# RWKV-7 in eight chunks of 64 on 64x64 tiles of the array, its transitions made for all chunks at once, and the round reordered

## What is computed

```
w = -softplus(-(w0 + tanh(w_lr) @ w2)) - 0.5;  decay = exp(-exp(w))
a = sigmoid(a0 + a_lr @ a2)
kk = k * k_k;  kk = kk / max(norm(kk), 1e-12);  k = k * (1 + (a - 1) * k_a)
for each token:
    sa = state @ (-kk)
    state = state * decay + sa (x) (kk * a) + v (x) k
    y = state @ r
y = (y - mean(y)) * rsqrt(var(y) + eps) * ln_g + ln_b + sum(r * k * r_k) * v
```

## Time and profile before

| what | before |
|---|---|
| median of 3 runs | 1454.38 us (1452.08 to 1454.99) |
| profiled execution | 1457.13 us, span 1455.2 us |
| mean granted TensorE clock | 0.977 of full speed |
| PE busy | 1343.1 us, 92% of the span |
| DVE busy | 792.6 us, 54% |
| ACT busy | 555.6 us, 38% |
| POOL busy | 618.2 us, 42% |
| first `low_rank` (pair 0) starts | 101.0 us after the span's start |
| one steady round, `low_rank` to `low_rank` | 105.4 us |
| last round, its `low_rank` to the output projection's first product | 83.9 us |

### The profile page before, as it was taken

One profiled execution on the slowest core, in us unless ns is written; L12 is line 12 of the kernel. 1 busy time (PEld: TensorE's weight loads), 2 busy tenths in 40 slices (PEclk: granted clock), 3 DMA queues, 4 the chain that ended last, 5 costly groups with the idle time before them and its releaser, 6 DMA issues.

```text
span 1455.2 us, 24702 instructions
## 1 busy us (share of the span) xinstructions
PE 1343.1 (92%) x7914; PEld 1096.5 (75%) x7914; DVE 792.6 (54%) x1442; ACT 555.6 (38%) x1210; POOL 618.2 (42%) x584
## 2 busy tenths in 40 slices
PE   2999999999999999999999979899969999998995
PEld 1777878878878878878878858687847777776874
DVE  6546256366275274374383462205584777687357
ACT  4324344344254245254244354202242425435123
POOL 3634233242242341350351211477745656565772
PEclk9999999999999999999999989899989999999998
DMA  5212011111021120120120110333312222222331
GB/s 179 86 48 56 23 50 48 30 46 43 29 54 35 36 59 22 43 59 14 43 67 7 43 37 15 108 109 96 93 58 80 80 73 80 75 77 56 99 92 65
DMA packets 46688, 87.81 MB, mean 60 GB/s; under 512 B 5808, under 2 KB 6832, under 8 KB 46384
## 3 DMA queue, kind: packets, MB, share of 16 engines
q1 hardware_dynamic: 44352, 82.44, 19.7%
q10 hardware_dynamic: 2288, 4.72, 0.9%
HBM read 85.04 MB, written 2.10 MB: 60 GB/s over the span
## 4 chain that ended last, share of the span: by engine, by line
PE 72%; DVE 13%; issue 4%; ACT 4%; ACTq 0%; DVEq 0%
PE psum L272 67%; PE psum L426 3%; ACT mix L844 3%; DVE mix L1284 2%; DVE mix L1374 1%; DVE mix L1308 1%; ACT L844 1%; PE psum L781 1%; DVE mix L1746 1%; DVE mix L1664 1%; PE psum L351 1%; DVE mix L1457 1%; DVE mix L1675 1%; DVE mix L1738 1%; DVE mix L1729 1%
## 5 line engine op out<-in xcount | busy, mean ns | idle before, releaser
L272 PE MATMUL psum<-h_split,w_hi 128*128 128x512 f32 x2320 | 746.9, 404 | 17.1 <-DVE h_split L1288 9.2
L255 POOL TENSOR_SCALAR w_hi<-w_raw 128x512 fp32r<-128x512 f32 x290 | 205.3, 708 | 786.8 <-PE psum L272 668.4
L272 PEld LDWEIGHTS psum<-h_split,w_hi 128*128 128x128 f32 x2320 | 436.0, 192 | 127.7 <-issue 33.0
L272 PE MATMUL psum<-h_split,w_lo 128*128 128x512 f32 x1160 | 458.4, 395 | 0.0
L272 PE MATMUL psum<-mix 128*128 128x128 f32 (+4 forms) x3712 | 429.4, 287 | 28.4 <-ACT mix L844 11.7
L272 PEld LDWEIGHTS psum<-mix 128*128 128x128 f32 (+2 forms) x3712 | 369.6, 176 | 80.5 <-issue 33.8
L257 POOL TENSOR_TENSOR w_lo<-w_raw,w_hi 128x512 fp32r<-128x512 f32 x290 | 413.4, 1426 | 24.2
L844 ACT ACTIVATE mix<-psum 128x256 f32<-128x256 f32 (+4 forms) x620 | 229.2, 390 | 433.2 <-PE psum L272 241.1
L272 PEld LDWEIGHTS psum<-h_split,w_lo 128*128 128x128 f32 x1160 | 221.8, 191 | 48.4
L1374 DVE COPY_PREDICATED mix<-mask,psum 128x128 f32<-128x128 uint8 (+3 forms) x344 | 133.0, 431 | 171.0 <-PE psum L272 166.4
L844 ACT ACTIVATE mix<-mix 128x512 f32<-128x512 f32 (+3 forms) x274 | 138.0, 539 | 157.0 <-DVE mix L1647 71.2
(11 more groups left out here) (116 smaller groups left out, 747.0 us busy)
## 6 DMA issues: line engine op xcount, KB each, us to landing
w_raw<-wall SPq DMA_DIRECT2D x290, 256.0 KB, 2.6
mix<-xT SPq DMA_DIRECT2D x4, 512.0 KB, 5.5
mix<-xT ACTq DMA_DIRECT2D x1, 2048.0 KB, 8.2
out<-mix SPq DMA_DIRECT2D x8, 256.0 KB, 2.1
mix<-mask_f SPq DMA_DIRECT2D x1, 1792.0 KB, 11.0
mix<-pT ACTq DMA_DIRECT2D x2, 512.0 KB, 3.4
mix<-lru_w ACTq DMA_DIRECT2D x4, 256.0 KB, 3.4
mix<-w2a ACTq DMA_DIRECT2D x16, 32.0 KB, 2.4
```

What stands on the lines that cost most here:

```text
L255: pool.tensor_scalar(w_hi[:, slot, :, :], w_raw[:, slot, :], 1.0, 0.0, ALU.mult, ALU.add).then_inc(sem["w_hi"], 1)
L272: return pe.matmul(o, lhsT, rhs, start=start, stop=stop, skip_group_check=True)
```

## The change

RWKV-7 now has RC = 8 chunks of RL = 64 tokens, and all its products but `low_rank`, the sums over heads and the chain work on 64x64 tiles of the array. For head e and parity g of the chunk, a product that reads partitions of head e and writes partitions of parity g uses one of four tiles. From `turned_products` and the masks on, a chunk's matrices lie on the partitions of its parity, so a product of the inverse reads and writes the same half (two tiles, on the diagonal). A group of such products is marked by one increment of a counter `tile_groups` ahead of it (51 in a round), for which nobody waits.

- The inverse has levels 1 to 5. N and its transposed form NT are both made by products (`inverse_n`, `inverse_nt`); no transposes are left, and NT is put in place by a masked copy on VectorE of its own.
- `token_rows` turns v, k, b and a by products with a 64x64 identity; that for v is with `centre`, which takes the mean over the head away, so `head_mean` goes.
- `solved_rows` applies the inverse to the right-hand sides of all chunks, `transitions` makes each chunk's transition and its readers, `state_sums` and `output_sums` collect what doesn't depend on the state. The chain is then six `hop`s: one product (128x128 weights, 64 columns) and on VectorE two `stt` each. `state_outputs` adds the states' part to the outputs.
- The gate tile is now `t(3)`. The round starts with `low_rank`; `head_var`, `pair_out` and `head_out` of the pair and head before are done in the next round's first part. `hg_norm` likewise.
- Units of weights, masks and parameters are laid out to match; layer 1 and the output projection are as before.

Functions and the new order on TensorE (in the last three lines VectorE's part of a hop):

```diff
+            def products(r, keys):
+
+                if keys is b_t:
+                    pe.wait_ge(sem["rw_ops"], count("rw_ops", r, 2))
+                    if not is_first(r):
+                        pe.wait_ge(sem["rw_norm"], count("rw_norm", r - 1, 0))
+                else:
+                    pe.wait_ge(sem["rw_masked"], count("rw_masked", r, 6))
+                pe.sem_inc(tile_groups, 1)
+                for p in range(4):
+                    for e in range(2):
+                        for g in range(2):
+                            c = 2 * p + g
+                            last = mm(bank[2 + e][rows[g], p * P:(p + 1) * P], keys[rows[e], tokens(c)], ar[rows[e], c, :, :])
+                last.then_inc(sem["rw_qk"], 1)
...
+            def in_group(grp):
+
+                return [(q, e, g, slice(64 * (2 * e + q), 64 * (2 * e + q) + 64)) for q in range(2) for e in range(2) for g in range(2)]
...
+            def inverse_n(r, lvl, grp):
+
+                pe.wait_ge(sem["rw_pev"], count("rw_pev", r, 2 * (lvl - 1) + grp))
+                if lvl == 1:
+                    pe.wait_ge(sem["rw_masked"], count("rw_masked", r, 4 + grp))
+                else:
+                    pe.wait_ge(sem["rw_xt"], count("rw_xt", r, 2 * (lvl - 2) + grp))
+                pe.sem_inc(tile_groups, 1)
+                for q, e, g, at in in_group(grp):
+                    last = mm(bank[4 + grp][rows[g], at], xinv_t[rows[g], grp, at], p_full[rows[g], grp, at])
+                last.then_inc(sem["rw_n"], 1)
...
+            def solved_rows(r, grp):
+
+                pe.wait_ge(sem["rw_xt"], count("rw_xt", r, 8 + grp))
+                if grp == 0:
+                    pe.wait_ge(sem["rw_ge"], count("rw_ge", r))
+                pe.sem_inc(tile_groups, 1)
+                for q, e, g, at in in_group(grp):
+                    n = 2 * (2 * e + q)
+                    last = mm(bank[4 + grp][rows[g], 64 * n:64 * n + P], xinv_t[rows[g], grp, at], ga[rows[g], e, 2 * grp + q, :, :])
+                last.then_inc(sem["rw_uw"], 1)
...
+            def transitions(r):
+
+                pe.wait_ge(sem["rw_ua"], count("rw_ua", r))
+                pe.wait_ge(sem["rw_ub"], count("rw_ub", r))
+                pe.sem_inc(tile_groups, 1)
+                for to, keys in ((6, 2), (4, 1)):
+                    for p in range(4):
+                        for g in range(2):
+                            for e in range(2):
+                                last = mm(bank[to + g][rows[e], 64 * p:64 * p + 64], uw[rows[g], p // 2, e, p % 2, 1, :],
+                                          rw_m[rows[g], e, p, keys, :])
+                    last.then_inc(sem["rw_mr"], 1)
...
-                t(0)
                 if pair:
                     low_rank(r)
-                t(1)
+                if first or not head:
+                    t(3)
+                t(0, 0, 4)
                 if pair:
                     key_norm(r)
+                    hg_norm(r)
+                t(0, 4, KC)
+                if pair and not is_first(r):
+                    head_var(r - 1)
+                t(1, 0, 4)
+                if pair:
                     bonus(r)
+                t(1, 4, KC)
+                t(2)
                 embedding(0)
-                t(2)
-                t(3)
+                embedding(1)
                 if pair:
-                    transposes(r)
-                    t(4, (0,))
-                    for c in range(CH):
-                        product(r, c)
-                    for c in range(CH - 1):
-                        inverse_start(r, c)
-                    t(4, (1,))
-                    inverse_start(r, 3)
-                    for lvl in range(1, 7):
-                        inverse(r, lvl)
-                    chain_rhs(r, 0)
-                    t(5, (0,))
-                    chain_u(r, 0)
-                    t(5, (1,))
-                    chain_out(r, 0)
-                else:
-                    t(4)
-                    t(5)
-                embedding(1)
+                    products(r, b_t)
+                    turned_products(r, head)
+                    token_rows(r, 0)
+                    token_rows(r, 1)
+                    inverse_p(r, 1, 0)
+                    token_rows(r, 2)
+                    token_rows(r, 3)
+                    inverse_p(r, 1, 1)
+                    products(r, k_t)
+                    inverse_n(r, 1, 0)
+                    inverse_nt(r, 1, 0)
+                    inverse_n(r, 1, 1)
+                    for lvl in range(2, 5):
+                        inverse_p(r, lvl, 0)
+                        if lvl == 4:
+                            value_rows(r)
+                        inverse_nt(r, lvl - 1, 1)
+                        inverse_p(r, lvl, 1)
+                        inverse_n(r, lvl, 0)
+                        inverse_nt(r, lvl, 0)
+                        inverse_n(r, lvl, 1)
+                    inverse_p(r, 5, 0)
+                    inverse_nt(r, 4, 1)
+                    inverse_p(r, 5, 1)
+                    state_sums(r, True)
+                    inverse_nt(r, 5, 0)
+                    inverse_nt(r, 5, 1)
+                    output_sums(r, True)
+                    solved_rows(r, 0)
+                    solved_rows(r, 1)
+                if head and not first:
+                    t(3, 0, 4)
+                embedding(2)
+                if pair:
+                    transitions(r)
+                    output_sums(r, False)
+                    state_sums(r, False)
+                if head and not first:
+                    t(3, 4, KC)
+                embedding(3)
+                for c in range(1, 5):
+                    if pair:
+                        hop(r, c)
+                    t(4, 2 * c - 2, 2 * c)
+                if pair:
+                    hop(r, 5)
+                level(0)
+                if pair:
+                    hop(r, 6)
+                level(1)
+                t(5, 0, 4)
+                if pair:
+                    state_outputs(r)
                 if head:
                     hg_values(i)
-                if pair:
-                    chain_rhs(r, 1)
-                level(0)
-                if pair:
-                    chain_u(r, 1)
-                level(1)
-                if pair:
-                    chain_out(r, 1)
-                embedding(2)
-                t(6)
-                if pair:
-                    chain_rhs(r, 2)
+                t(5, 4, KC)
                 level(2)
-                if pair:
-                    chain_u(r, 2)
                 level(3)
-                if pair:
-                    chain_out(r, 2)
-                embedding(3)
-                t(7)
-                if pair:
-                    chain_rhs(r, 3)
+                t(6, 0, 4)
                 level(4)
-                if pair:
-                    chain_u(r, 3)
+                t(6, 4, KC)
                 level(5)
-                if pair:
-                    chain_out(r, 3)
+                t(7, 0, 4)
                 level(6)
                 if head:
                     hg_diagonal(i)
                     hg_keys(i)
-                if pair:
-                    head_mean(r)
+                t(7, 4, 6)
                 if head:
                     hg_changes(i)
+                t(7, 6, KC)
+                if head:
                     hg_outputs(i)
-                if pair:
-                    head_var(r)
-                if head:
-                    hg_norm(i)
 
...
+                stt(s_next, state(c), e_pos[:, c, RL:RL + 1], n_add[:, c, :], ALU.mult, ALU.add).then_inc(sem["rw_z"], 1)
+                dve.wait_ge(sem["rw_z"], count("rw_z", r, c - 1))
+                dve.wait_ge(sem["rw_c"], count("rw_c", r, c - 1))
+                stt(s_all[:, c + 1, :], R1[:, 0:64], e_pos[:, c, RL:RL + 1], s_next, ALU.mult, ALU.add).then_inc(sem["rw_s"], 1)
```

More of the change, by code:

```diff
@@ new lines, in even_round @@
+                if pair:
+                    token_rows(r, 0)
+                    token_rows(r, 1)
+                    inverse_p(r, 1, 0)
+                    token_rows(r, 2)
+                    token_rows(r, 3)
+                    inverse_p(r, 1, 1)
+                    for lvl in range(2, 6):
+                        inverse_p(r, lvl, 0)
+                        if lvl == 4:
+                            value_rows(r)
+                        inverse_p(r, lvl, 1)
+                    solved_rows(r)
@@ L1096, in even_round @@
[L1096 to L1103 removed]
+                        for c in range(3, 6):
+                            high(c)
+                        embedding_tiles(0, 3, U_PRJ0, (0, 1))
@@ L1582, in even_round @@
+                    gated(i, 2, "sig_ga", sig_a, g_a)
                 if pair:
[L1583 to L1594 removed]
+                    dve.wait_ge(sem["rw_reset"], count("rw_reset", r))
@@ new lines, in even_round @@
+                    inverse_nt(r, 4, 1)
+                    inverse_nt(r, 5, 0)
```

(17 more changed lines are left out.)

940 lines of the change are left out of this document (467 added, 473 removed).

## The result

The changed kernel takes 1428.92 us (median of 4 runs, 1427.74 to 1430.82) beside 1453.7 of the kernel before: ratio 0.9832, 95% interval 0.9819 to 0.9844. That is 25 us less where 82 were forecast: inside the stated range, outside the forecast's own 1345 to 1400, and under a third of the move. The profiled execution's span went from 1455.2 to 1428.0, and the output projection's first product from 922.76 to 895.12, so all 27.6 us come from the rounds.

What follows compares the result with a forecast made beforehand. TensorE's work bounds the kernel; rounds of 105.4 us become 96.7. Seven rounds save 61, the earlier start 9, the last round 12: 82 less, median 1372; the forecast's own range is 1345 to 1400, the stated range 1322 to 1432.

Steps and rivals of the forecast that it cites:

- The work: TensorE's products per round: 38.7 us removed, 28.4 added, so its work falls by 10.3 us.
- Levels: Each inverse level on TensorE: 96 records at 0.029, 2.8 us in place of 4.45.
- the rival of diagonal tiles that go one after the other: Diagonal groups sharing a bank run serially at 0.058 a record, 15.7 us more a round: 1497; chance 0.08.
- the first rival: All four tiles run side by side (0.0145 a record) and no clock is lost: 1326; chance 0.2.
- What waits: List of TensorE's waits, clock loss, mode changes and gaps in a round: 10.8 us against 9.2 before.
- first gaps, the loop: 1.8: Per round on TensorE, mode changes, first gaps of groups and the loop together: 1.8 us.
- wait at t(2): TensorE waits at t(2) for VectorE's gated(i, 0): 3 to 7 us a round, taken as 5.0.
- slow clock behind it: Clock falls after the idle time at t(2): 1.3 us a round charged (0 to 3.4).
- wait ahead of turned_products: turned_products waits for gated(i, 2), through ScalarE's sigmoid and VectorE, with products beside it: 0.7 us a round.
- waits in the hops: Hops' hand-overs of 0.95 each, mostly covered by quarter tiles, with VectorE's HGRN2 levels between: 2.0 us a round.
- four-tile records: 352 records of 64 columns alternating over four tiles, at 0.025 each: 8.8 us a round (5.1 to 10.2).
- The rival of groups that cost more than their products: 51 increments and some 60 waits a round on TensorE's queue, 0.13 us a group: 6.6 a round, 1425; chance 0.12.

Runs made afterwards that it cites:

- e7: Changed kernel with TensorE's rounds written out, pair_out and bonus behind gated(0), t(3) chunks in the inverse, and q's sigmoid written to hq: 1357.04 us.
- e1: Changed kernel with TensorE's rounds 2 to 7 written out instead of looping, other engines keeping their loops: 1400.96 us, ratio 0.9628.
- e9: e7 without the tile_groups increments, their waits moved to each group's first product: 1348.06 us, ratio 0.9278.
- e10: e7 with TensorE's rounds 2 to 7 in the hardware loop again: 1395.64 us, ratio 0.9606.
- the padded kernels: Kernel before with 2, 4, 6 or 10 unused semaphore increments ahead of each projection chunk in TensorE's loop: 1455.09, 1489.37, 1555.09, 1780.8 us.
- e2: Changed kernel with VectorE's pair_out and bonus moved from right before gated(i, 0) to right after it: 1418.6 us, ratio 0.9743.

## Why the prediction was wrong

**The work, right.** Levels take what was forecast: in e7, a group of 96 records

```profile
499.68 3.02 PE L320 MATMUL psum<-mix 64*64 64x64 f32 x96
```

has steps of (3.02 - 0.22)/95 = 0.029, so the rival of diagonal tiles that go one after the other is out. The Trainium skill, TensorEngine Tiling (Array Packing), Restrictions and Gotchas, says that row tiles can't use one bank at a time; the measured step here is half of the 0.054 that a record of 64 columns would take with nothing beside it (an estimate from the 0.43 of a 512-column fp32 record), and the measurement decides. Four alternating tiles take (2.10 - 0.22)/127 = 0.0148 a record (the row at 353.06), the rate of the first rival, where I took 0.025: 3.6 us a round better.

**What waits, wrong, in the step that lists it.** That list has hand-overs, mode changes and "first gaps, the loop: 1.8"; nowhere did it ask whether TensorE has its instructions. Against it, for a steady round (295.31 to 400.02, 104.7; forecast 96.7):

| item | forecast | measured |
|---|---|---|
| taken branch | in 1.8 | 4.3 |
| half clock behind it | 0 | 2.6 |
| waits for blocks in the inverse | 0 | 3.2 |
| wait at t(2) | 5.0 | 2.9 |
| slow clock behind it | 1.3 | 1.7 |
| wait ahead of turned_products | 0.7 | 0.55 |
| waits in the hops | 2.0 | 0.95 |
| wait of hg_outputs on the states (L1515) | 0 | 0.95 |
| four-tile records | 8.8 | 5.2 |

The differences sum to +4.3 + 2.6 + 3.2 - 2.1 + 0.4 - 0.15 - 1.05 + 0.95 - 3.6 = 4.55; 3.45 of the 8.0 aren't split. The t(2) row looks like a wait that was forecast too long and isn't: VectorE used the time of the branch, 4.6 us ahead of this round. The half clock's 2.6 are the 6.40 us from low_rank's start to key_norm's (301.71 - 295.31) less the 3.8 priced for that piece. Without a branch the wait is 4.27 (e1), close to my 5.0, but by a chain through ScalarE and its table that I hadn't drawn. In the total, five turns are 8.2 above forecast (41), rounds 1 and 7 together 8, the last round 7.7 (a wait of 9.55 for gated(3), which holds the first embedding, and 4 us of block waits), and the start is 2.5 better: 54.2, and 82 - 54.2 = 27.8, for 27.6 measured.

The rival of groups that cost more than their products gave 1425, close to the time measured, but not its cause: the marks that it priced at 53 us in all gave 9 when they were taken off (e9).

**What the profile offered.** The row of the old kernel's instruction queue, 32 blocks, with none moving in five rounds, and the order, which shows 1267 products' records where 697 stood, were both there. The Trainium skill, in the section on instruction fetch named above, says that a taken branch out of the two blocks held stalls on a fetch. It would have pointed at this wait, though by two blocks the old loop would have stalled as well, and its branch took 0.21. That each cause is one is shown by e1 and e10 (branch), the padded kernels (the length alone), and e2 and e7 (t(2)). That the regular waits of 0.2 to 1.2 us in the inverse are blocks arriving late rests on the traces. In the changed kernel all 40 issue waits over 0.2 us from 80 to 930 us, but for those at the branch and one that ends 0.10 us after a gated, end 1.2 to 1.6 us after a block's landing; in the stretches without a branch they stand whole multiples of 256 instructions apart, within 2. The blocks themselves start 3.8 to 5.0 us apart in the inverse of the round from 295.31. No run removed the waits alone. Why a block doesn't come sooner stays open.

## What to carry to other kernels

Count TensorE's instructions in a hardware loop, weight load and matmul apart and fp32 twice, and look at the instruction row of the DMA queues: when a loop outgrows what the engine holds, each turn pays several us that no hand-over explains, and writing the loop out is then the cheaper form. Issue waits that stand 256 instructions apart are the same supply running late. When many short products replace few long ones, price the instructions as well as the columns. A wait that looks as long as forecast may be a longer one that another stall has covered; remove the stall and measure it again, and follow its chain through every engine that touches the buffer.

## What the runs showed of the hardware

- TensorE kept a loop of 1686 instructions and not one of 1814; a taken branch takes 0.21 to 0.24 us in the first case and 3.3 to 5.7 in the other (1814 to 2664 instructions; the longest in e2).
- A semaphore increment on TensorE's queue costs nothing at 2 for three 512-column products, and 0.147 us each from 6 to 10.
- 64x64 fp32 products of 64 columns at full clock: 0.029 us a record on two diagonal tiles that write one bank, 0.0148 on four.
- Waits for instructions in runs of 64x64, 64-column fp32 products stand 256 TensorE instructions apart, or a multiple, and end 1.2 to 1.6 us after a 16 KB block has landed.
- Granted clock after a wait at t(2) with tiles on both sides: below 1.00 in two of five rounds after 2.00 us (e2, 0.67 over the 5.2 us that follow), in four of five after 2.90 (0.69 to 0.70 over 5.5), and 0.50 right after each of the five idle times of 4.3 to 4.7 at the branch.
